# Matmuls of constants in TensorE's waits: one layer of a hybrid attention, linear-attention and mixture-of-experts model

## The reference

```python
mod = silu(cond) @ w_ada + b_ada          # 6 x 1024 values per stream (latent, context)
h = LN(x) * (1 + sc1) + sh1
proj = h @ w_in                           # q, k, v of attention; q, k, v, r of GLA; gates
merged = g_a * (attention(...) @ w_br_attn) + g_b * (gla(...) @ w_br_gla)
x = LN(alpha * x + g1 * (merged @ w_out)) * ln1_g + ln1_b
h2 = LN(x) * (1 + sc2) + sh2
# routing: best of 4 groups, then best 2 of its 8 experts; 32 experts of width 256
y = sum over the 2 chosen e of w_e * ((silu(h2 @ gate_e) * (h2 @ up_e)) @ down_e)
x = LN(alpha * x + g2 * y) * ln2_g + ln2_b
```

## Time and profile before

| what | value |
|---|---|
| time before, median of 3 runs | 726.18 us (726.13 to 726.43) |
| the profiled execution's own time | 725.1 us |
| its span in the profile | 723.3 us |
| PE busy | 639.7 us (88%), 3233 matmul records |
| DVE, ACT, POOL busy | 276.1, 109.7, 113.6 us |
| DMA | 176.60 MB, mean 244 GB/s |
| mean granted clock of TensorE | 0.942 |

### The profile page before, as it was taken

The page is one execution under the profiler, slowest core; times in us unless marked ns, Lnnn a source line. Parts: engine busy times, 40 slices in busy tenths (PEclk is TensorE's granted clock), DMA queues, the critical chain, the costliest instruction groups (busy, mean ns, idle before and its releaser), DMA issues.

```text
span 723.3 us, 8214 instructions
## 1 busy us (share of the span) xinstructions
PE 639.7 (88%) x3233; PEld 346.8 (48%) x3233; DVE 276.1 (38%) x568; ACT 109.7 (15%) x227; POOL 113.6 (16%) x116
## 2 busy tenths in 40 slices
PE   1699998999999999999999946999997888887895
PEld 0274345554444455564444545666664545444331
DVE  2422443236743553132226754233332222224217
ACT  0020442210022221124000011111110000010000
POOL 3000000010300000000002223233333222221100
PEclk9799999999999999999999965999999888899898
DMA  9979426036333030239965194799999999999532
GB/s 335 369 238 315 164 106 232 30 110 221 129 117 101 15 117 16 101 116 302 387 247 198 58 396 172 285 406 405 405 404 407 405 402 401 406 402 407 207 144 87
DMA packets 67495, 176.60 MB, mean 244 GB/s; under 512 B 10420, under 2 KB 12500, under 8 KB 67456
## 3 DMA queue, kind: packets, MB, share of 16 engines
q1 hardware_dynamic: 50832, 143.56, 52.1%
q10 hardware_dynamic: 10880, 24.21, 9.4%
q0 software_dynamic: 5744, 8.28, 3.3%
HBM read 174.55 MB, written 11.96 MB: 258 GB/s over the span
## 4 chain that ended last, share of the span: by engine, by line
PE 73%; DMA 14%; SPq 5%; DVE 4%; issue 2%; ACT 1%; POOL 0%; DVEq 0%; POOLq 0%
PE bank L1522 25%; PE bank L1777 11%; DMA X<-exp_w_up 6%; PE bank L1694 6%; PE bank L1708 6%; PE bank L1785 5%; DMA W<-exp_w_up 3%; DMA X<-w_ada 3%; SPq L449 2%; PE bank L1474 2%; DMA Y<-exp_w_down 2%; PE bank L1652 2%; PE bank L1670 2%; PE bank L1893 2%; PE bank L1763 1%
## 5 line engine op out<-in xcount | busy, mean ns | idle before, releaser
L1522 PE MATMUL bank<-W,Y 128*128 128x512 f32 (+1 forms) x432 | 183.7, 579 | 0.0
L1522 PEld LDWEIGHTS bank<-W,Y 128*128 128x128 f32 x432 | 80.7, 192 | 86.0 <-issue 83.7
L1777 PE MATMUL bank<-X,Y 128*64 128x256 f32 x704 | 86.4, 401 | 10.2 <-DMA X<-exp_w_up 9.4
L1777 PEld LDWEIGHTS bank<-X,Y 128*64 128x64 f32 x704 | 55.6, 144 | 46.9 <-DMA X<-exp_w_up 17.4
L633 POOL TENSOR_TENSOR rstd<-ss,cst 128x1 f32<-128x1 f32 (+3 forms) x21 | 22.6, 1074 | 348.0 <-DVE ss L784 348.0
L677 POOL DMA_INDIRECT Y<-h_rows,gidx x32 | 41.4, 1293 | 106.4 <-PE bank L1763 95.0
L1163 DVE COPY abias<-bank 128x128 f32<-128x128 f32 x32 | 9.3, 291 | 122.0 <-PE bank L1807 122.0
L1777 PE MATMUL bank<-W,Y 128*64 128x256 f32 (+1 forms) x320 | 39.7, 368 | 10.6 <-DMA Y<-exp_w_up 6.1
L682 POOL DMA_INDIRECT pair_rows<-PTr,sidx x32 | 32.9, 1029 | 64.1 <-DVE PTr L1181 63.5
L1785 PE MATMUL bank<-X,abias 128*64 128x512 f32 x176 | 42.6, 603 | 0.4 <-issue 0.4
L1694 PE MATMUL bank<-W,Y 128*128 128x512 f32 x96 | 42.0, 594 | 0.3 <-PE bank L1694 0.3
(11 more groups left out here) (228 smaller groups left out, 711.5 us busy)
## 6 DMA issues: line engine op xcount, KB each, us to landing
X<-exp_w_gate SPq DMA_DIRECT2D x22, 1024.0 KB
X<-exp_w_up SPq DMA_DIRECT2D x22, 1024.0 KB
X<-exp_w_down SPq DMA_DIRECT2D x22, 1024.0 KB, 19.8
W<-w_in SPq DMA_DIRECT2D x8, 2048.0 KB, 8.6
Y<-w_ada ACTq DMA_DIRECT2D x8, 2048.0 KB, 9.2
W<-exp_w_gate SPq DMA_DIRECT2D x10, 1024.0 KB, 18.3
W<-exp_w_up SPq DMA_DIRECT2D x5, 1024.0 KB
W<-exp_w_down SPq DMA_DIRECT2D x5, 1024.0 KB
```

Of the source, the lines that this page charges most:

```text
L1522: ins = mm(bank[:, 0:cols], hT[:, i, k, :], w[:, k, :], start=k == 0, stop=k == KT - 1)
L1777: ins = mm(bank[hh * 64:hh * 64 + 64, a:b], x_[:, c, h * 64:h * 64 + 64], rhs(hh), start=k == 0 and a == 0, stop=k == KT - 1, skip_group_c ...
```

## The change

A helper `keep_busy(count)` issues `count` matmuls of the identity with 512 columns of the constants into `banks[6]`. Their result isn't read by anybody, and the next real user of the bank starts a new sum. The helper is called at eight places of TensorE's stream.

```diff
+FILL_START = (5, 7, 3, 3)
+FILL_NORM, FILL_ROUTER, FILL_RANK, FILL_GATHER = 4, 5, 2, 5
...
+            def keep_busy(count):
+
+                for _ in range(count):
+                    mm(banks[6][:, :], ident, cst[:, 0:HALF], start=True, stop=True)
+
             pe.wait_ge(S["consts_in"], 16)
+            keep_busy(FILL_START[0])
             pe.wait_ge(S["cond_silu"], 2)
             colbank = side.claim(pe, "modc", 0)
             for n in range(4):
+                if n:
+                    keep_busy(FILL_START[n])
                 modulation(n)
                 if n:
                     columns(colbank, 8 * (n - 1), n - 1)
...
             for i in range(TILES):
+                if i == TILES - 1:
+                    keep_busy(FILL_NORM)
                 second_transposes(i)
...
             main.filled(ins, "router")
+            keep_busy(FILL_ROUTER)
             pe.wait_ge(S["both_ready"], 1)
...
             side.filled(ins, "count")
+            keep_busy(FILL_RANK)
             main.wait_read(pe, "wo", 0, TILES - 1)
...
             index_tables(0)
+            keep_busy(FILL_GATHER)
             next_tokens(0)
```

## The result

The changed kernel took 722.51 us (median of 7 runs, 718.25 to 725.83), against 726.13 (722.95 to 726.43) of the kernel before beside it: a ratio of 0.9944 [0.992, 0.9968]. So the change makes the kernel faster by 0.6 to 0.7%, about half of the 1.3% forecast, and the first median lies 1.0 us above the range. The profiled execution took 718.25 us, with a span of 716.5 us.

The account below looks back on a forecast made before the run. Five stages bound the span, with the saturated DMA weight stream starting behind `gate_up(0)`; 1.7 us at the start and 8.0 in the routing give 9.7, so 725.1 becomes 715.4 profiled, 716.5 as a median (-1.3%), range 713.5 to 721.5.

Parts of the forecast that it names:

- The stages and their joints: Whole span: five stages with different limits; bringing expert 0's gate_up forward brings the DMA-saturated weight stream forward by as much.
- rival D: DMA stream: its end is set by something that doesn't move with its start; 724.5 to 726 us, chance 0.05.
- The cost of the added matmuls: Eight waits of TensorE: 34 matmuls at 0.86 us each at full clock, 1.7 at half; none late beyond a few tenths.
- Rival C: Start and routing: added matmuls don't raise the clock and outlast their waits; up to 754 us, chance 0.05.
- Terms 2 to 7: Routing, from the third tile's transposes to expert 0's gate_up: TensorE's work at full clock saves 8.0 us.
- rival A: Routing: narrow matmuls let the clock fall again, losing 3 to 4 us of 8.0; 719 to 722 us, chance 0.18.
- The rule that was weighed: Routing: transposes don't count as busy time in the same way; taken strictly, gains from third tile to index table shrink.
- Terms 2 to 4: Routing at full clock: third tile's transposes and router save 2.1 us, ranks 0.7, index table 1.35.
- Term 1: Start: block 3 begins at its landing and takes 1.92 us in place of 3.60; 1.7 us, bounds 0 and 2.3.
- Rival B: Start gives nothing: block 4 or kvl's weights land when they did before; only 8.0 us gained, 718.2 us, chance 0.12.

Follow-up runs that it names:

- tiny: Kernel before plus 18 two-column matmuls at the start (6 ahead of block 0, 12 ahead of block 1), no routing fills: 726.89 us against 725.45, 1.0012.
- again: The changed kernel unaltered, in a second, longer comparison: 720.0 us against 725.76 of the kernel before, ratio 0.9926.
- route_only: The changed kernel without the start fills, only those of norm, router, rank and gather: 719.4 us against 725.76, ratio 0.9915.
- rank_gather: The changed kernel with only the rank and gather fills (2 and 5), none at start, norm or router: 724.34 us against 726.15, ratio 0.999.
- route_tight: The changed kernel without start fills, routing fills 4, 6, 2, 6 in place of 4, 5, 2, 5: 719.44 us against 725.74, ratio 0.9909.
- tight_again: route_tight once more for a second profile, one execution: 720.18 us.
- narrow: The changed kernel without start fills, routing fills 8, 10, 3, 10 of 36 columns in place of 512: 726.07 us against 725.94, ratio 0.9999.
- ada4_early: The full change with block 4's load issued when VectorE has read block 2 instead of block 3: 721.04 us against 725.94, ratio 0.9936.
- half_wide: The changed kernel without start fills, routing fills 2, 3, 1, 3 in place of 4, 5, 2, 5: 722.73 us against 725.94, ratio 0.9961.
- start_13: The full change with start fills 4, 4, 2, 3 in place of 5, 7, 3, 3: 719.22 us against 726.15, ratio 0.992.

## Why the prediction was wrong, and what in it was right

**The stages and their joints: right.** From the first waiting load to the end of the span it is 267.3 us before, 267.1 after, and 266.7 to 269.2 in all twenty profiles, though the load moves from 459.50 (`tiny`) to 447.56 (`again`). The saturated stream moves as a whole with `gate_up(0)`, and rival D is out.

**The cost of the added matmuls: right at full clock.** 0.45 us a record in a row of ten (4.54), forecast 0.43. The first five began with the landing of the constants at 4.98 us and took 6.68, so block 0 began at 11.59 in place of 11.25 and took 1.92; the forecast had them end at 12 or 13. At full clock they were hidden, in the changed kernel's profile, but for 0.4 us ahead of each of blocks 2 and 3, within the 0.5 us that was allowed. The cover is gone where it isn't, as the prediction said: 3.66 us in the rank fill of `route_only`, 3.76 in that of `rank_gather`. Rival C as a whole is out: identity and constants raise the clock.

**Terms 2 to 7, 8.0 us: right in size, wrong as an expectation.** The table of pieces gives 7.8 in `again`, each term within 0.3 us. What failed is the step "If the clock stays at 1.00 through the waits", which had a chance of 0.60. The clock fell for 3.4 us in the routing in eight of ten profiles, and in three of ten, one of them without such a fall, SyncE went on 1.3 to 1.5 us late. So 0.9 to 2.4 us were lost in nine of ten, and what is left, 6.1 us as a mean, is in the main rival A at a smaller price than its 3 to 4 us. `route_tight` and `tight_again` have less idle time between the fills and the full amount in both profiles; two profiles aren't many, since two of the ten kept the clock as well.

The rule that was weighed is the Trainium skill's, in TensorE: Matmul & The Clock Gate, Part 4, that transposes don't bring the full clock. As to raising it the trace agrees, and `narrow` shows the same for plain 36-column matmuls (0.50 in both windows above, ratio 0.9999). As to holding it, transposes and router of the third tile run at full pace from 422.63 to 425.95 in `again`. Terms 2 to 4 did not shrink as the strict reading would have it.

**Not all of the loss is a fall that the records show.** In the changed kernel's profile `gate_up(0)` has its full pace, 3.67 us to 447.94, and yet SyncE goes on only at 449.45, and ScalarE, which waits for the same matmuls, with it; in `again` it was at once. TensorE in windows of 1 us, changed kernel:

```profile
448.00:449.00 1.00, 0.62 (x4) 0.43 (x4) 0.00 (x0) 0.00 (x0) 0.24 (x1) 1.00 0.04 8
449.00:450.00 1.00, 0.00 (x0) 0.00 (x0) 0.24 (x1) 0.55 (x2) 0.00 (x0) 1.00 0.21 62
```

TensorE has already done the next transposes, and nobody else moves until 449.45. The changed kernel's four other profiles don't have this gap, so it belongs to the execution and not to the kernel. The same gap, 1.26 to 1.51 us, is in five profiles (this one, `ada4_early`, `half_wide`, `start_13`, `rank_gather`), none of which shows 0.50 in `gate_up(0)`; in the other fifteen it is 0.04 us. `ada4_early`, `gate_up(0)` and SyncE's load:

```profile
443.80 3.67 PE L1794 MATMUL bank<-X,Y 128*64 128x256 f32 x32
```

```profile
448.74 0.37 SPq L453 DMA_DIRECT2D X<-exp_w_gate  x1
```

The gap is about what a fall of the clock costs in `gate_up(0)` in other profiles (1.7 us). Ends of matmuls are modelled in the profile, so it may be such a fall that the records don't show; no run settles this.

**Term 1, 1.7 us: wrong, it is 0.** Two steps failed. One is "Block 3 starts with its landing at 31.63 as before and takes 1.92 us in place of 3.60": it starts 0.9 us later as a mean, and it took 2.9 us, not 3.60, as a mean of the profiles without fills, so nothing is gained at its end (34.4 us with fills, 34.5 without). Transposes at full clock still bring the end of the second `kvl` projection forward by 1.4 us. The other is "The load moves forward by the same 1.7 us as block 3": block 4's load took 1.9 us longer in the changed kernel's profile than in the one before and landed 0.8 us later, and later by 1.1 us as a mean. Rival B said this and had 0.12. The later landing of block 3, in five of the seven, stands beside an instruction fetch that the prediction didn't reckon with; it said that "No DMA queue, no other engine and no semaphore is passed or added", but the profile lists the fetch among the DMA queues.

**The sum.** 725.1 - 6.1 - 0 = 719.0 for a profiled execution; the five profiled executions of the changed kernel took 717.7 to 720.1 us, so it is met. Since the 6.1 us are read from the runs, this is a check of the account and not of the forecast. Rivals A and B held together, which the prediction priced only apart: 718.2 by B and 1.9 us less gain by A make 720.1. What it doesn't explain is the long side: timed executions reach 726.01, and the first median is 722.51. There is no trace of those, but the longer spans tend to have the lower mean clock: of the six others of the first comparison whose span and clock are known, the longest has 724.1 us at 0.967 and the shortest 717.4 at 0.979, though one of 721.2 has 0.979 too. By (1 - clock) x 2 x span that is 48 us at 0.50 against 30. Where these stretches lie, the runs don't show. The prediction named such falls in its last lines and didn't widen the range for them.

**What stays open:** the cause of the late signal behind `gate_up(0)`, why the early fetch goes with a late block 3 in six profiles and not in three, why block 4's load takes longer, and the place of the extra time at low clock in the longer executions. No version tried is shown to be better than the change: `route_only`, `route_tight` and `start_13` are at 719.2 to 719.4, the full change at 720.0, and their intervals overlap. The fills at the start can be left out. The gain of 8.0 us in the routing was never seen in a timed median, only in the rows of single profiles.

## What to carry to other kernels

In this kernel idle waits cost twice, since narrow work followed them at the lower clock; a few unread 512-column matmuls in the waits of a chain that sets the end took most of that back. Each group should be slightly shorter than its wait at full clock, with no wait ahead of it left unfilled. Price the gain by the terms, but take the mean over several profiles, since the clock's falls come at different places from one execution to the next. Take the old cost of a step from several profiles too: block 3 alone varied from 1.92 to 3.64 us. And where the DMA engines are saturated, look where the instruction fetches move.

## What the runs showed of the hardware

- Matmuls of 36 columns kept TensorE busy 8.7 to 8.9 of 10 us and the granted clock stayed at 0.50; a row of 512-column matmuls with constants as operands, begun at 0.50 at 436.96 us in `rank_gather`, had `gate_up(0)` at full pace at 449.78 (3.67 us).
- An instruction fetch is one packet of 16 KB that holds one of the 16 DMA engines for 1.1 us. 72 more instructions moved it forward to 29.6 us (`tiny`), from between 35.5 and 36.3 us. Of the nine profiles in which it came ahead of the landing of a 2 MB weight block, six had that landing about 1.1 us later and three did not.
- `pe.nop()`, written 72 times, left the page's instruction count at 8214 and the fetch where it was.
- Two engines can see TensorE's signal 1.3 to 1.5 us after the last of its records ends (five of twenty profiles), with the clock printed as 1.00 at that place; in the other fifteen SyncE goes on 0.04 us after it.
- With the 4, 5, 2, 5 fills the granted clock was at 0.50 in the routing for 3.4 us in eight profiles and not at all in two; without them it was at 0.50 for 34 us (421 to 455 us in the kernel before).
